# Linear attention in two chunks of 128 without a carried state, and a new order on VectorE around the triangular inverse

## The reference

```
log_a = log_sigmoid(a_low @ w_a_up + b_a) / 16
b = cumsum(log_a) inside each chunk                    # the reference's chunks have 64 tokens
att = (q exp(b)) (k exp(-b))^T, causal                 # inside the chunk
o = att v + (q exp(b)) state                           # state: what earlier chunks left
state = exp(b_last) state + (k exp(b_last - b))^T v    # handed from chunk to chunk
```

## Time and profile before

| | us |
|---|---|
| median of 3 runs | 887.34 (886.88 to 888.05) |
| the profiled execution | 886.68 |
| its span, first to last instruction | 884.6 |
| PE busy | 868.8 (98%) |
| VectorE busy | 586.7 (66%) |
| ScalarE busy | 441.4 (50%) |

### The profile page before, as it was taken

How to read it: one execution, slowest core, us unless ns; L and a number is a source line. 1 busy time by engine, 2 the same in 40 slices (tenths; PEclk the granted TensorE clock), 3 DMA queues, 4 the chain that set the end, 5 groups by cost and what they waited for, 6 DMA issues and landing times.

```text
span 884.6 us, 13530 instructions
## 1 busy us (share of the span) xinstructions
PE 868.8 (98%) x5486; PEld 751.0 (85%) x5486; DVE 586.7 (66%) x900; ACT 441.4 (50%) x647; POOL 56.1 (6%) x81
## 2 busy tenths in 40 slices
PE   8999999999999999999999999899999999999997
PEld 6888999898889888888889998677888888888885
DVE  5785665565656656565686999766477677777544
ACT  6644444654355544544475652456353655555442
POOL 1000000000020100000020015200000100000000
PEclk9999999999999999999999999999999999999999
DMA  9757744445455555466748783312455555665441
GB/s 287 247 191 212 238 144 144 143 145 189 143 149 184 191 157 176 149 205 194 275 110 275 188 163 123 106 50 49 143 190 191 182 181 186 190 191 190 166 167 48
DMA packets 124772, 151.56 MB, mean 171 GB/s; under 512 B 15991, under 2 KB 88054, under 8 KB 124710
## 3 DMA queue, kind: packets, MB, share of 16 engines
q1 hardware_dynamic: 124426, 150.34, 54.4%
q10 hardware_dynamic: 220, 0.28, 0.1%
q0 software_dynamic: 64, 0.07, 0.0%
HBM read 148.57 MB, written 3.68 MB: 172 GB/s over the span
## 4 chain that ended last, share of the span: by engine, by line
PE 92%; DVE 4%; ACT 2%; issue 1%; DMA 1%; POOL 0%; POOLq 0%; SPq 0%; ACTq 0%; DVEq 0%
PE bank L525 19%; PE bank L527 19%; PE bank L526 19%; PE bank L1344 9%; PE bank L551 5%; PE bank L1345 5%; PE bank L552 3%; PE bank L1002 1%; PE bank L743 1%; PE bank L723 1%; PE bank L840 1%; DVE w_lo L2136 1%; DMA arena<-in_x 1%; PE bank L703 0%; PE bank L1095 0%
## 5 line engine op out<-in xcount | busy, mean ns | idle before, releaser
L2136 DVE TENSOR_TENSOR w_lo<-ring,w_hi 128x2048 fp32r<-128x2048 f32 (+2 forms) x134 | 297.6, 2225 | 131.2 <-ACT w_hi L1551 130.8
L1551 ACT ACTIVATE w_hi<-ring 128x2048 fp32r<-128x2048 f32 (+2 forms) x134 | 249.0, 1861 | 110.7 <-PE bank L527 81.9
L1344 PE MATMUL bank<-h_both,w_hi 128*128 128x512 f32 x352 | 124.8, 399 | 0.2 <-issue 0.2
L525 PE MATMUL bank<-h_both,w_hi 128*128 128x256 f32 x424 | 122.3, 289 | 0.0
L526 PE MATMUL bank<-h_both,w_hi 128*128 128x256 f32 x424 | 119.9, 283 | 0.0
L527 PE MATMUL bank<-h_both,w_lo 128*128 128x256 f32 x424 | 119.9, 283 | 0.0
L1345 PE MATMUL bank<-h_both,w_lo 128*128 128x256 f32 x352 | 98.8, 281 | 0.0
L525 PE MATMUL bank<-w_hi,h_both 128*128 128x512 f32 (+2 forms) x224 | 86.2, 385 | 0.0
L527 PE MATMUL bank<-w_hi,h_both 128*128 128x512 f32 (+2 forms) x224 | 84.1, 376 | 0.0
L526 PE MATMUL bank<-w_lo,h_both 128*128 128x512 f32 (+2 forms) x224 | 84.1, 375 | 0.0
L525 PEld LDWEIGHTS bank<-h_both,w_hi 128*128 128x128 f32 x424 | 81.2, 192 | 1.9 <-issue 1.5
(11 more groups left out here) (385 smaller groups left out, 1526.5 us busy)
## 6 DMA issues: line engine op xcount, KB each, us to landing
ring<-in_w_in SPq DMA_DIRECT2D x59, 1024.0 KB, 5.2
ring<-in_w_gate_up SPq DMA_DIRECT2D x44, 512.0 KB, 4.7
ring<-in_w_down SPq DMA_DIRECT2D x10, 1024.0 KB, 5.1
ring<-in_w_mem_kv SPq DMA_DIRECT2D x8, 1024.0 KB, 9.8
ring<-in_w_gla_out SPq DMA_DIRECT2D x4, 1024.0 KB, 5.0
ring<-in_w_x_out SPq DMA_DIRECT2D x4, 1024.0 KB, 5.2
ring<-in_w_dsa_out SPq DMA_DIRECT2D x4, 1024.0 KB, 5.3
ring<-in_w_o SPq DMA_DIRECT2D x4, 1024.0 KB, 5.0
```

The costliest lines, as they stand in the source:

```text
L525: mm(o, ah, bh, start=start, stop=False, skip_group_check=True)
L1344: mm(o[:, :], wh[:, k - k0, w], h_both[:, :, k, :], start=k == 0, stop=False, skip_group_check=True)
L1551: act(w_hi[:, k % NHI, at:m], ring[:, order.index(name) % NSLOT, at:m], ACT.Copy)\
L2136: tt_(w_lo[:, i, at:m], ring[:, i, at:m], w_hi[:, k % NHI, at:m].bitcast(F), ALU.subtract)\
```

## The change

GLA: the running sum restarts every 128 tokens in place of 64, so there are two chunks, and no state is formed. The first chunk's output is its masked scores by its values. The second's is its own masked scores by its values, and a second score matrix by the first chunk's values: `k_end` (keys of the first chunk, decayed to its end) by `q_start` (queries of the second, decayed from its start), one product `at2` of four heads, which ScalarE copies to `att_before`. As sums over 128 tokens reach further, the exponents inside a chunk are taken relative to the chunk's 64th token (`gate_mid`). The key transposes, the `k^T v` products, the states and their VectorE additions are gone.

Second block: `shifted_blocks` works on both halves at once (8 instructions for 16). On VectorE it is followed at once by `Tm` and `turned`; the rotations, scaled keys and values come behind them. On PE the wait for the rotations stands behind `level(1)` and `hidden_sum`. The low parts of `z0` and `z1` are held back: `z0` is split behind the first four `nsa_scores`, `z1` behind `compressed_max`.

```diff
-    put("keep", np.broadcast_to(np.arange(S) % CH != 0, (128, S)))
+    put("keep", np.broadcast_to(np.arange(S) % 128 != 0, (128, S)))
+    put("causal", p <= f)
-        first_at = region(384)
+        first_at = region(512)
...
             pe.wait_ge(signal("gla_kt"), 1)
-            for j in range(TT):
-                bank = open_bank(f"kt{j}")
-                for h in range(H1):
-                    ins = nc.tensor.transpose(bank[:, 128 * h:128 * h + 128], gk[:, h, 128 * j:128 * j + 128], ident)
-                done(f"kt{j}", ins)
+            bank = open_bank("at2")
+            for h in range(H1):
+                ins = mm(bank[:, 128 * h:128 * h + 128], k_end[:, h, :], q_start[:, h, :], start=True, stop=True)
+            done("at2", ins)
             wide_tokens("zg0", h_parts)
-            for t, chunks in enumerate(((0, 1), (2,))):
...
-                            ins = mm(bank_of(f"kv{c}{j}")[:, 256 * hh:256 * hh + 256], kt_tok[r:r + 64, 4 * t + h, :],
-                                     gv[r:r + 64, t, 256 * h:256 * h + 256], start=True, stop=True)
...
             wide_tokens("zg1", h_parts)
             pe.wait_ge(*read("at1"))
+            pe.wait_ge(*read("at2"))
             for h in range(H1):
...
-                    ins = mm(bank_of(f"og{h}")[r:r + 64, a:a + 256], gq[:, h, 64 * c:64 * c + 64],
-                             state[c - 1][:, 256 * h:256 * h + 256], start=False, stop=True, skip_group_check=True)
+                bank, v = open_bank(f"og{h}"), slice(256 * h, 256 * h + 256)
+                mm(bank[:, 0:256], attT[:, h, :], gv[:, 0, v], start=True, stop=False, skip_group_check=True)
+                mm(bank[:, 256:512], attT[:, 4 + h, :], gv[:, 1, v], start=False, stop=False, skip_group_check=True)
+                ins = mm(bank[:, 256:512], att_before[:, h, :], gv[:, 0, v], start=False, stop=True, skip_group_check=True)
                 done(f"og{h}", ins)
...
-            pe.wait_ge(signal("rope_done"), 4)
             level(1)
             hidden_sum()
+            pe.wait_ge(signal("rope_done"), 4)
             nsa_logits(0)
...
-                    sp.wait_ge(*full("kt1"))
+                    sp.wait_ge(*full("at2"))
...
-            act(cumlog, expo, ACT.Exp, scale=1 / 16).then_inc(signal("gate_exp"), 1)
-            act(k_d, expo, ACT.Exp, scale=-1 / 16).then_inc(signal("gate_exp"), 1)
-            act(decay1.rearrange("p (h c) -> p h c", h=4),
-                expo.rearrange("p h (c t) -> p h c t", t=CH)[:, :, :, CH - 1], ACT.Exp, scale=1 / 16)
+            act(q_start, expo[:, :, 128:256], ACT.Exp, scale=1 / 16).then_inc(signal("gate_exp"), 1)
+            sc.wait_ge(signal("gate_mid"), 1)
+            act(k_d, cumlog, ACT.Exp, scale=-1 / 16).then_inc(signal("gate_exp"), 1)
+            act(cumlog, cumlog, ACT.Exp, scale=1 / 16).then_inc(signal("gate_exp"), 1)
...
+            tt_(cumlog.rearrange("p h (c t) -> p (h c) t", t=128), b, b[:, :, CH - 1:CH].broadcast_to([128, 8, 128]),
+                ALU.subtract).then_inc(signal("gate_mid"), 1)
             cross_gate(1)
...
-            for c in range(NCH - 1):
-                for j in range(2):
-                    bank_ready(f"kv{c}{j}")
...
-                            ins = nc.vector.tensor_copy(state[0][:, s], src)
-                        else:
-                            ins = stt(state[c][:, s], state[c - 1][:, s], decay1[:, 4 * h + c:4 * h + c + 1], src,
-                                      ALU.mult, ALU.add)
...
-                            for half in range(2):
-                                ins = tt_(dst[:, 8 * half:8 * half + 8, :], t_[:, q::2, half:half + 15],
-                                          cmp_pos[kv][r, 8 * half:8 * half + 8].unsqueeze(2).broadcast_to([64, 8, 15]), ALU.add)
+                            t_ = bass.AP(b.tensor, b.offset + q, [list(b.ap[0]), [16, 2], [2, 8], [16, 15]])
+                            dst = cblk[kv][r, :, 15 * g:15 * g + 15].rearrange("p (f s) n -> p f s n", f=2)
+                            pos = cmp_pos[kv][r, :].rearrange("p (f s) -> p f s", f=2)
+                            ins = tt_(dst, t_, pos.unsqueeze(3).broadcast_to([64, 2, 8, 15]), ALU.add)
...
             lows(splits_by["kg1"] + 2)
+            ahead[0] = splits.index("nq1") + 1
...
             shifted_blocks()
+            ib = const("id64").unsqueeze(1).broadcast_to([128, 8, CH])
+            ve.wait_ge(signal("level_mask"), 1)
+            tt_(Tm, nAm[0], ib, ALU.add).then_inc(signal("T_start"), 1)
+            ve.wait_ge(signal("T_start"), 1)
+            turned(TmT, Tm)
+            rope_sin(2, 4, 2)
+            rope_add(2, 4, 2)
...
-            rope_sin(2, 4, 2)
-            lows(splits_by["vt1"] + 2)
...
-            rope_add(2, 4, 2)
             rope_add(3, 6, 2)
-            ahead[0] = splits.index("z1") + 1
...
             for i in range(4):
                 nsa_scores(i)
+            ahead[0] = splits.index("z0") + 1
+            lows(ahead[0])
             nsa_norm(0)
             nsa_norm(1)
             level_add(1)
             compressed_max()
+            ahead[0] = splits.index("z1") + 1
```

More of the change, by code:

```diff
@@ L55, in _const_columns @@
     at = 0
-    for name, width in (("ident", 128), ("diag3", 384), ("keep", S), ("chunk", 128), ("bucket", 383), ("pad", 1),
+    for name, width in (("ident", 128), ("diag3", 384), ("keep", S), ("chunk", 128), ("bucket", 383), ("pad", 1), ("causal", 128),
                         ("lev", 6 * 64), ("id64", 64), ("chunk64", 64), ("after", 128), ("rope", 128), ("cos", S), ("sin", S), ("selg", 256),
@@ L285, in build @@
         cumlog, expo = tiled(xq_at, 4, S), tiled(xq_at + 1024, 4, S)
-        state = (flat(xq_at, 1024), flat(xq_at + 1024, 1024), flat(mk_at + 1024, 1024))
         k_d = tiled(mk_at, 4, S)
-        kt_tok, expo_last = tiled(mv_at, 8, 128), flat(mv_at + 1024, 1024)
+        att_before, k_end, q_start = tiled(mv_at, 4, 128), tiled(mv_at + 1024, 4, 128), tiled(mk_at + 1024, 4, 128)
         gq, gk = tiled(gq_at, 4, S), tiled(gk_at, 4, S)
@@ L805, in _ @@
+            for h in range(H1):
+                ins = mm(bank[:, 128 * h:128 * h + 128], k_end[:, h, :], q_start[:, h, :], start=True, stop=True)
+            done("at2", ins)
+            wide_tokens("zg0", h_parts)
             wide_tokens("zg1", h_parts)
             pe.wait_ge(*read("at1"))
+            pe.wait_ge(*read("at2"))
             for h in range(H1):
-                bank = open_bank(f"og{h}")
-                for t in range(TT):
-                    mm(bank[:, 256 * t:256 * t + 256], attT[:, 4 * t + h, :], gv[:, t, 256 * h:256 * h + 256],
-                       start=t == 0, stop=False, skip_group_check=True)
@@ L812, in _ @@
-            pe.wait_ge(*read("kv21"))
-            for h in range(H1):
-                for c in range(1, NCH):
-                    r, a = 64 * (c % 2), 256 * (c // 2)
-                    ins = mm(bank_of(f"og{h}")[r:r + 64, a:a + 256], gq[:, h, 64 * c:64 * c + 64],
-                             state[c - 1][:, 256 * h:256 * h + 256], start=False, stop=True, skip_group_check=True)
+                bank, v = open_bank(f"og{h}"), slice(256 * h, 256 * h + 256)
+                mm(bank[:, 0:256], attT[:, h, :], gv[:, 0, v], start=True, stop=False, skip_group_check=True)
@@ L1700, in _ @@
                 copy_aside(f"dq{j}", dq[:, 2 * j:2 * j + 2, :])
-            for j in range(TT):
-                copy(f"kt{j}", kt_tok[:, 4 * j:4 * j + 4, :].rearrange("p a b -> p (a b)"))
+            copy("at2", att_before.rearrange("p a b -> p (a b)"))
             for c, t in itertools.product(range(2), range(TT)):
@@ L2314, in _ @@
             ve.wait_ge(*read("gk1"))
-            ve.wait_ge(signal("gate_cum"), 1)
-            last = expo.rearrange("p h (c t) -> p (h c) t", t=CH)[:, :, CH - 1:CH].broadcast_to([128, 16, CH])
-            tt_(expo_last.rearrange("p (a t) -> p a t", t=CH), last, expo.rearrange("p h (c t) -> p (h c) t", t=CH),
-                ALU.subtract).then_inc(signal("gate_diff"), 1)
+            tt_(k_end, expo[:, :, 127:128].broadcast_to([128, 4, 128]), expo[:, :, 0:128], ALU.subtract)\
+                .then_inc(signal("gate_diff"), 1)
             lows(splits_by["gv11"] + 2)
-            ve.wait_ge(signal("gate_exp"), 2)
+            ve.wait_ge(signal("gate_exp"), 3)
+            step(stt(q_start, gq[:, :, 128:256], DK ** -0.5, q_start, ALU.mult, ALU.mult))
             stt(gq, gq, DK ** -0.5, cumlog, ALU.mult, ALU.mult)
@@ L2638, in _, with turned @@
             shifted_blocks()
+            def turned(dst, src):
+                nc.vector.transpose(dst.rearrange("p a b -> p (a b)"), src.rearrange("p a b -> p (a b)"))\
+                    .then_inc(signal("T_turned"), 1)
+            ib = const("id64").unsqueeze(1).broadcast_to([128, 8, CH])
[5 more added lines that the diff above has]
+            rope_add(2, 4, 2)
             for t in range(TT):
@@ L2650, in _ @@
             rope_sin(3, 6, 2)
-            rope_add(2, 4, 2)
```

(9 more changed lines are left out.)

33 lines of the change are left out of this document (8 added, 25 removed).

## The result

The changed kernel took 876.64 us (median of four runs, 874.65 to 878.09) beside 887.11 (886.68 to 888.05) for the kernel before: a ratio of 0.9879, 95% interval [0.9858, 0.99]. A second set on another chip gave 876.74 against 887.90, 0.9874 [0.9859, 0.9889]. The forecast of 878.6 had the direction and both places, and was 2.0 us too high; the result lies at the very low edge of its range, 876.6, which the forecast reached only with all its terms at their best ends.

What follows compares the result with a forecast made beforehand. The prediction took PE, busy for 98% of the span, as the bound. Linear attention -5.5, the inverse -3.4 and constants +0.2 gave -8.7, so 878.0 us and, 0.66 higher for the median, 878.6; range 876.6 to 881.3.

Steps and rivals of the forecast that it cites:

- GLA on PE, -5.5: Linear attention on PE: products removed, minus the added output products, save 5.5 us, with bounds -6.4 to -4.6.
- All of it on the path: Linear attention: PE runs there without idle, so all the removed work, 5.5 us, pulls the rest forward.
- rival 2: Linear attention: loads or splits feed PE too late and half the gain is lost; -5.9 in all, 881.4 us; chance 0.07.
- The constants, +0.2: Kernel start: 64 KB more of constants load ahead of the first memory unit, costing 0.2 us (0 to 0.4).
- The stall goes whole, -3.4: First level of the inverse: the turned matrix is ready before PE asks, so PE's wait disappears, saving 3.4 us.
- The wait for the rotations next, 0 to 0.1: Ahead of the logits: PE's next late input is the rotations, for which it waits 0 to 0.1 us.
- `z0`'s split uncovered by 0.4, the clock giving back 0.4, the two cancelling: Before the first norm: the moved split costs 0.4 us, faster logits return 0.4, so the second level stays at -3.4.
- The rule weighed beside it: Logits behind the inverse: without PE's idle the full 0.87 us of slow clock comes back, making the sum some 0.4 lower.
- `z1`'s split covered: Ahead of the fifth row's scores: the 2.28 us split is caught up within VectorE's later idle of 6.05 us.
- rival 1: NSA rows: VectorE becomes the bound because of the split of `z1`; 2.28 us come back, -6.4, 880.9 us; chance 0.13.
- rival 3: Linear attention's gate: ScalarE and VectorE wait on each other, two units' splits come late, 11.1 us lost, 889.7 us; chance 0.04.
- From the span to the median: Whole kernel: -8.7 from the profiled 886.68 gives 878.0 us; 0.66 is added for the median, giving 878.6.

Runs made afterwards that it cites:

- GLA alone: The kernel before with only the linear attention and its constants taken from the changed kernel: 881.05 us, ratio 0.9923.
- start matrix late: The changed kernel with `Tm` and `turned` back behind the rotations, scaled keys and values; the splits stay held back: 880.11 us.
- the wait ahead: The changed kernel with PE's wait for the rotations back ahead of the first level: 878.64 us.
- both splits early: The changed kernel with the splits of `z0` and `z1` back where they stood in the kernel before: 876.26 us.
- sixteen: The changed kernel with the shifted additions in sixteen instructions, as in the kernel before: 876.78 us.
- `z0` early: The changed kernel with the split of `z0` alone back in its early place, that of `z1` staying late: 875.85 us, ratio 0.9865.
- order alone: The kernel before with only the second half of the change (order around the inverse, eight shifted additions, splits held back): 883.38 us, ratio 0.995.
- the halves behind the scores: The changed kernel with the split of `z0` cut in two, behind the fourth row's scores and behind the first level's sum: 876.35 us.
- the changed kernel run again: The changed kernel once more, unaltered, timed beside the kernel before: 876.74 us.
- `z0`'s split in halves: The changed kernel with the split of `z0` cut in two, ahead of the hidden product and behind the fourth row's scores: 876.76 us.

## Why the prediction was right in kind and 2 us too high

- *GLA on PE, -5.5.* Right in kind, too small: -6.05 at `zd0`. `k^T v`: from the first `zg0` product to `og` there were 248.41 - 222.60 = 25.81 us and now there are 244.68 - 222.79 = 21.89, so 3.92 and not 3.65 went. The group also slowed the wide products next to it: the first one behind it took 237.69 - 237.35 = 0.34 us up to the next start, where further on they stand 0.23 apart. Output: twelve products took 249.67 - 244.68 = 4.99, 0.208 a record, where the sum had 0.221. `at2` for the transposes: +0.02 (0.79 to 0.81). The bounds, -6.4 to -4.6, held it.
- *All of it on the path; rival 2.* Right, and rival 2 fell: GLA alone keeps 5.5 to the end of its span.
- *The constants, +0.2.* Not shown. The start moved by 0.17, within what equal kernels show.
- *The stall goes whole, -3.4.* Right: the hidden products are 5.77 earlier, the first level 9.21, so 3.44. The turned matrix stood at 540.1. The stall needs the start matrix ahead (start matrix late, +3.4) and the wait for the rotations behind the first level (the wait ahead, 1.31 us of stall); it does not need the splits held back (both splits early) or the eight additions (sixteen).
- *The wait for the rotations next, 0 to 0.1.* Right: the sum ends at 548.15, the logits start at 548.48. Moving that wait was worth 1.9.
- *`z0`'s split uncovered by 0.4, the clock giving back 0.4, the two cancelling.* This step failed. Its sum took the split's cover, VectorE's idle of 1.87 us, from the stage as it ran at half the clock, and let the clock's return move VectorE's scores but not the exponentials that VectorE waits for. The clock gave 1.49: between the first level and the compressed scores the shift grows from 9.21 to 10.70. The logits gave 1.15 of it (from their start to the next product 560.36 - 557.70 = 2.66 before, 549.99 - 548.48 = 1.51 after), since the price per record was taken from the length of a later group of eight; the rest came in the compressed keys behind them, which the sum left out. ScalarE's exponentials came 10.70 earlier with them, so the idle that was to cover the split shrank to 1.08 (`z0` early), and the split cost 1.0. The stretch from the compressed scores to the second level shows both prices. It is 3.08 to 3.09 where no split stands in it (before, GLA alone, `z0` early), 3.32 and 3.36 with the split behind slow logits (start matrix late, the wait ahead), and 4.11 with it at the full clock (changed, order alone). So the sum's 0.4 is near what the split costs at the low clock, 0.25, and the change itself took that away. The sign that the prediction named, the split ending about when the exponentials do, did not come true: it ended a microsecond behind them. The stage came to -3.9 in place of -3.4, so two errors of 1.1 and 0.6 partly hid each other. That part is luck.
- *The rule weighed beside it.* By the Trainium skill ("TensorE: Matmul & The Clock Gate", Part 1) an idle PE is put to half its clock and gets it back by being busy, from which the prediction worked out that the whole loss comes back. The trace agrees, with 0.50 behind the idle and 1.00 without it, and that sum, 0.4 lower, would have been nearer.
- *`z1`'s split covered; rival 1.* The rival was wrong for this kernel: the idle that the forecast named shrank by 2.1. It is real one step on, when the second level is 1.0 earlier (0.61 us in the halves behind the scores).
- *The gate's mutual waits; rival 3.* Wrong: `zg0` starts 0.19 later, the scores ahead of it 0.17.
- *From the span to the median.* This step failed too, and it is the largest term. Forecast -8.7, spans -9.6. The profiled run of before, 886.68, lies at the low end of its runs, and 0.66 was added for that to the changed kernel too, for which no row spoke; its profile of 876.77 lies on its median of 876.74. That and a gap of 1.77 in place of 2.08 between span and time make 1.0. Why the runs of the kernel before lie above its profile is open: the nine in the set of the changed kernel run again show a mean clock of 0.994 to 0.996 against 0.997 in the profile, the changed kernel's four beside them 0.998 to 0.999. But two runs of the kernel before with 0.994 took 886.5 too, so the mean clock alone does not explain it, and only profiled executions have a trace.

What failed is thus the carried offset, by 1.0, with its cause open; the price of the GLA's records, by 0.5; and the step on `z0`'s split and the clock, by 0.5 net, whose cause the experiments show.

## What to carry to other kernels

Price a stall of TensorE with what it slows behind it: here 3.4 us of idle cost some 1.5 more at half the clock, and 1.3 us of idle cost 1.6 more up to the compressed scores. When a change speeds up a stage, read the cover for moved work from the stage as it will be: the gap ahead of the first norm was 1.87 us in the slow stage and 1.08 in the fast one. When work is to leave a critical stretch, ask first which single instruction the waiting engine needs and move that one; the split of `z0`, moved as well, had been filling an idle time, and its new place cost 1.0. Before filling a gap on VectorE, look whether GpSimd works beside it.

## What was not expected of the hardware

- An idle of 1.31 us on PE was followed by a granted clock of 0.50 for the logits (2.86 us in place of 1.58); behind 0.83 and 0.68 us of idle in the changed kernel the same kind of products, eight records, took 0.93 as in the kernel before.
- The lower clock came only once PE worked again: in the kernel before the profile shows 1.00 in the idle and from 556 to 557 us, 0.97 from 557 to 558, and then 0.50 from 558 to 561.
- A VectorE subtraction of 128x1024 took 2.28 us beside GpSimd's products and 1.18 to 1.22 without (`z0`'s split in halves, both ways).
- The pace of 352 equal products was 399 ns in twelve profiles and 393 in one, at a granted clock of 1.00 in both.
